# Attention with a log-multiplicity mask, sums from the exponential and inverse sums on the diagonal of the turning product; inject and lag stages reordered

## What is computed

```python
h = rmsnorm(x); u, q, k, v = split(h @ w_in)        # 4 x 1024 columns
y = Re(C x) + D u, x = complex diagonal scan of B u # 64 groups, state 64
z = gelu(y); z = z * sigmoid(z @ w_glu)
for window, dilation in ((128, 1), (512, 4), (2048, 16)):
    o_i, lse_i = softmax attention over t, t-d, .., t-window
o = sum(softmax(lse)_i * o_i)                       # 8 heads of 128
x = x + concat(rmsnorm(z), rmsnorm(o)) @ w_out
x = x + hierarchical_moe(rmsnorm(x))                # 32 SwiGLU experts, top 2
```

## Time and profile before

| | before |
|---|---|
| runs, us | 2140.65, 2148.05, 2150.82 |
| profiled execution, us | 2141.37 |
| its span, us | 2139.6 |
| mean granted clock of PE | 0.931 |
| busy: PE, DVE, ACT, POOL | 83%, 27%, 15%, 13% |
| chain of work that ended last: DMA, PE, DVE | 37%, 30%, 6% |
| read from HBM | 517.78 MB |

### The profile page before, as it was taken

One profiled execution on the slowest core, in us unless ns is written; L12 is line 12 of the kernel. 1 busy time (PEld: TensorE's weight loads), 2 busy tenths in 40 slices (PEclk: granted clock), 3 DMA queues, 4 the chain that ended last, 5 costly groups with the idle time before them and its releaser, 6 DMA issues.

```text
span 2139.6 us, 26995 instructions
## 1 busy us (share of the span) xinstructions
PE 1772.0 (83%) x10906; PEld 1240.1 (58%) x10907; DVE 579.4 (27%) x1218; ACT 312.2 (15%) x505; POOL 273.9 (13%) x193
## 2 busy tenths in 40 slices
PE   7997999898559999997687787877877797977780
PEld 6887888787337888886444444444444454544440
DVE  6300899822976520002300000000000000000006
ACT  4002211002232201111110110101101010111012
POOL 0641322101920000000100000000000000000000
PEclk9998999999689999998799999989999999999996
DMA  5245212335904422332799999999999689899995
GB/s 226 79 116 121 70 62 116 118 137 148 6 28 153 176 100 83 133 119 72 313 395 411 400 422 400 407 388 396 411 401 393 269 331 413 335 404 417 409 420 223
DMA packets 92405, 536.13 MB, mean 251 GB/s; under 512 B 28760, under 2 KB 41560, under 8 KB 47256
## 3 DMA queue, kind: packets, MB, share of 16 engines
q1 hardware_dynamic: 74528, 514.07, 63.3%
q0 software_dynamic: 7776, 17.07, 2.6%
q10 hardware_dynamic: 10048, 4.23, 1.0%
HBM read 517.78 MB, written 30.91 MB: 256 GB/s over the span
## 4 chain that ended last, share of the span: by engine, by line
DMA 37%; PE 30%; DVE 6%; issue 2%; ACT 1%; SPq 0%; POOLq 0%; ACTq 0%; DVEq 0%
DMA arena<-w_up_in 35%; PE psum L528 13%; PE psum L797 10%; PE psum L813 2%; DVE arena L1300 1%; DMA arena<-y_rows 1%; PE psum L654 1%; DVE arena L1294 1%; DVE arena L1292 1%; PE psum L660 1%; PE psum L777 1%; PE psum L722 1%; DVE arena L1552 1%; DVE arena L1545 0%; DMA y_rows<-arena 0%
## 5 line engine op out<-in xcount | busy, mean ns | idle before, releaser
L528 PE MATMUL psum<-arena 128*128 128x260 f32 x3328 | 744.8, 387 | 26.5 <-ACT arena L835 13.0
L528 PEld LDWEIGHTS psum<-arena 128*128 128x128 f32 x3328 | 639.1, 192 | 128.3 <-issue 19.3
L797 PE MATMUL psum<-arena 128*64 128x256 f32 x4352 | 538.9, 406 | 178.5 <-DMA arena<-w_up_in 142.0
L797 PEld LDWEIGHTS psum<-arena 128*64 128x64 f32 x4352 | 331.0, 146 | 396.5 <-DMA arena<-w_up_in 166.1
L1538 DVE TENSOR_TENSOR arena<-arena,psum 128x256 f32<-128x256 f32 x34 | 14.3, 421 | 953.5 <-PE psum L797 953.5
L813 PE MATMUL psum<-arena 128*64 128x512 f32 x1088 | 245.4, 603 | 20.4 <-ACT arena L994 15.6
L813 PEld LDWEIGHTS psum<-arena 128*64 128x64 f32 x1088 | 75.6, 138 | 168.3 <-issue 131.8
L1110 POOL DMA_INDIRECT y_rows<-arena x34 | 34.0, 1000 | 979.0 <-ACT arena L999 934.1
L994 ACT ACTIVATE arena<-psum 128x256 f32<-128x256 f32 x34 | 13.1, 384 | 496.8 <-PE psum L803 496.8
L777 PEld LDWEIGHTS psum<-arena 64*128 64x128 f32 x560 | 64.9, 203 | 22.1 <-issue 22.1
L777 PE MATMUL psum<-arena 64*128 64x64 f32 x560 | 69.7, 276 | 8.9 <-ACT arena L985 8.9
(11 more groups left out here) (295 smaller groups left out, 1127.2 us busy)
## 6 DMA issues: line engine op xcount, KB each, us to landing
arena<-w_down_in SPq DMA_DIRECT2D x64, 2048.0 KB, 27.3
arena<-w_gate_in SPq DMA_DIRECT2D x64, 2048.0 KB, 28.0
arena<-w_up_in SPq DMA_DIRECT2D x64, 2048.0 KB
arena<-w_in_in SPq DMA_DIRECT2D x32, 1024.0 KB, 4.8
arena<-w_out_in SPq DMA_DIRECT2D x16, 1024.0 KB, 4.8
arena<-k_cache_in SPq DMA_DIRECT2D x8, 1024.0 KB, 6.7
arena<-v_cache_in SPq DMA_DIRECT2D x8, 1024.0 KB, 4.8
arena<-y_rows SPq DMA_DIRECT2D x8, 1024.0 KB, 8.2
```

The costliest lines, as they stand in the source:

```text
L528: last = mm(pair(n)[:, h, :], w(kk), rhs(kk)[:, HALF * h:HALF * (h + 1)], start=(kk == begin), stop=(kk == kn - 1 and stop))
L797: last = mm(ps[64 * h:64 * h + 64, i // 2, 0:256], xtr[:, kk, :], w[:, kk, 256 * h:256 * (h + 1)], start=(kk == 0), stop=(kk == 15))
```

## The change

It does these things:

- The constant is one table, -log(n), with 1e30 where n is 0. DVE's mask becomes table - SCALE x scores, its minimum is the bias, and ACT exponentiates with scale -1, so n is inside the exponential. The exponential also gives the sum. DVE only inverts it; ACT writes the inverse on a diagonal (`inv_l`), and PE turns the weights by a real product with that diagonal instead of a transpose.
- ACT's copy of the turned weights and PE's weighing stand one step later.
- Rounds 0 and 1 of the weight stacks are issued by POOL.
- Key chunks go with tiles 26 to 31, and the last two behind them.
- `ssm_c` is loaded ahead of the stores of k and v; POOL waits for `bst` only at the last of the four powers, and uses another buffer for intermediate results until then.
- The lag kernels are made, copied and given their diagonal in two halves, and PE starts on a channel tile when its part is ready.
- Two semaphores that did nothing go.

```diff
--- before
+++ after
...
@@ -379,9 +380,11 @@
                         if keys is not None:
                             if a > keys:
                                 sp.wait_ge(s_ku, it * 2 + (j - 2 * keys - 1))
-                            sp.dma_start(kch[j].rearrange("p k d -> p (k d)"),
-                                         t["k_cache"][bass.ds(it * 2 + (j - 2 * keys), 1)].rearrange(
-                                             "o p n -> (o p) n")).then_inc(s_kch[j], 16)
+                            load_keys(j, it * 2 + (j - 2 * keys), 1)
+
+            def load_keys(j, c, n):
+                sp.dma_start(kch[j].rearrange("p k d -> p (k d)"),
+                             t["k_cache"][bass.ds(c, n)].rearrange("o p n -> (o p) n")).then_inc(s_kch[j], 16)
 
             load_tiles(2, 6)
             for rd in (2, 3):
...
@@ -393,13 +396,18 @@
                                      ).then_inc(s_bs[rd], 16)
             load_tiles(6, 8)
             sp.wait_ge(s_inj, 24)
-            sp.dma_start(view(tail, 1024), t["c_branch"]).then_inc(s_attc, 16)
+            sp.dma_start(branch, t["c_branch"]).then_inc(s_attc, 16)
             sp.dma_start(smp_const, t["c_sample"]).then_inc(s_sc, 16)
-            load_tiles(8, 11)
-            load_tiles(11, 12, 11)
-            load_tiles(12, 15, 11)
-            load_tiles(15, 16)
-
+            load_tiles(8, 13)
+            load_tiles(13, 14, 13)
+            load_tiles(14, 16, 13)
+            for c in (6, 7):
+                sp.wait_ge(s_ku, c - 1)
+                load_keys(c % 2, c, 1)
+
+            sp.wait_ge(s_proj, 32)
+            sp.wait_ge(s_state, 1)
+            sp.dma_start(cw[:, 0], t["ssm_c"]).then_inc(s_c, 16)
             sp.wait_ge(s_rope, 16)
             sp.dma_start(t["k_out"], k).then_inc(s_kout, 16)
             sp.wait_ge(s_rope, 24)
...
@@ -410,9 +418,6 @@
             sp.dma_start(router_const, t["c_router"]).then_inc(s_rc, 16)
             sp.dma_start(region("upper", P), t["c_upper"]).then_inc(s_rc, 16)
 
-            sp.wait_ge(s_proj, 32)
-            sp.wait_ge(s_state, 1)
-            sp.dma_start(cw[:, 0], t["ssm_c"]).then_inc(s_c, 16)
             sp.wait_ge(s_vout, 16)
             sp.wait_ge(s_vr, 8)
             sp.wait_ge(s_vs, 1)
...
@@ -611,7 +616,8 @@
                 if a >= 2:
                     pe.wait_ge(s_ptev, a - 1)
                 for j in range(a % 4 + 1):
-                    last = pe.transpose(ps[:, 4 + a % 2, P * j:P * (j + 1)], sc[a % 4][:, P * j:P * (j + 1)], ident)
+                    last = mm(ps[:, 4 + a % 2, P * j:P * (j + 1)], sc[a % 4][:, P * j:P * (j + 1)], inv_l[:, a % 4],
+                              start=True, stop=True)
                 last.then_inc(s_pt, 1)
 
             def weigh(h):
...
@@ -631,8 +637,9 @@
                 if a + 4 < 4 * NH:
                     scores(a + 4)
                 turn(a)
-                if a % 4 == 3:
-                    weigh(a // 4)
+                if a % 4 == 0 and a:
+                    weigh(a // 4 - 1)
+            weigh(NH - 1)
 
             pe.wait_ge(s_cw, 1)
             pe.wait_ge(s_msk, 4 * NH)
...
@@ -642,12 +649,13 @@
                         last = mm(ps[32 * r:32 * r + 32, ct // 4, P * (ct % 4):P * (ct % 4 + 1)].rearrange(
                             "p (j m) -> p j m", j=CHUNK), bst[:, ri, 4 * ct + r, :], cw[:, 0:CHUNK, ri, 4 * ct + r, :],
                             start=(ri == 0), stop=(ri == 1))
-            last.then_inc(s_lag, 1)
-
-            pe.wait_ge(s_lagd, 1)
+                if ct % 4 == 3:
+                    last.then_inc(s_lag, 1)
+
             pe.wait_ge(s_state, 1)
             for ct in range(8):
                 b = ct % 2
+                pe.wait_ge(s_lagd, ct + 1)
                 if ct >= 2:
                     pe.wait_ge(s_z, ct - 1)
                 for lag in range(CHUNK):
...
@@ -660,6 +668,8 @@
                             mm(yjc[b][32 * r:32 * r + 32, j, :], cw[:, j + 1, ri, i, :], xs[:, ri, i, 0:NCH],
                                start=False, stop=(j == CHUNK - 1 and ri == 1), skip_group_check=True)
                 ys = ps[:, 2 * b + 1, 0:NS]
+                if ct == 0:
+                    pe.wait_ge(s_lagc, 3)
                 mm(ys, lagk[:, ct, 0, :], u[:, ct, SEQ:T], start=True, stop=False, skip_group_check=True)
                 for ri in range(2):
                     for r in range(4):
...
@@ -845,13 +855,6 @@
             A(tmp[5], tmp[4], ACT.Sin).then_inc(s_lact, 1)
             A(tmp[6], tmp[4], ACT.Sin, scale=0.5).then_inc(s_lact, 1)
 
-            def stack_weights(rd):
-                for r in range(4):
-                    for j in range(CHUNK):
-                        act.dma_start(bws[rd % 2][32 * j:32 * j + 32, :, r, :],
-                                      bw[32 * r:32 * r + 32, CHUNK - 1 - j, rd // 2, 4 * (rd % 2):4 * (rd % 2) + 4, :]
-                                      ).then_inc(s_bs[rd], 16)
-
             def chunk_states(rd):
 
                 for b in range(6):
...
@@ -896,7 +896,12 @@
             def exps(a):
                 act.wait_ge(s_mx, a + 1)
                 w = P * (a % 4 + 1)
-                A(sc[a % 4][:, 0:w], sc[a % 4][:, 0:w], ACT.Exp, bias=stat[:, a:a + 1], scale=SCALE).then_inc(s_exp, 1)
+                A(sc[a % 4][:, 0:w], sc[a % 4][:, 0:w], ACT.Exp, bias=stat[:, a:a + 1], scale=-1.0,
+                  accum_out=stat[:, 32 + a % 4:33 + a % 4]).then_inc(s_exp, 1)
+
+            def diagonal(a):
+                act.wait_ge(s_inv, a + 1)
+                A(inv_l[:, a % 4], ident, ACT.Copy, scale=stat[:, 36 + a % 4:37 + a % 4]).then_inc(s_p, 1)
 
             def turned(a):
                 act.wait_ge(s_pt, a + 1)
...
@@ -914,17 +919,21 @@
             for a in range(4 * NH):
                 if a + 1 < 4 * NH:
                     exps(a + 1)
-                turned(a)
+                diagonal(a)
+                if a:
+                    turned(a - 1)
                 if a % 4 == 1 and a > 4:
                     head_out(a // 4 - 1)
+            turned(4 * NH - 1)
             head_out(NH - 1)
 
-            act.wait_ge(s_lag, 1)
             act.wait_ge(s_lagc, 1)
-            for r in range(4):
-                last = A(lagk[32 * r:32 * r + 32, :, :, 32 * r:32 * r + 32],
-                         psum_t[32 * r:32 * r + 32, 0:1024].rearrange("p (c j m) -> p c j m", c=8, j=CHUNK), ACT.Copy)
-            last.then_inc(s_lagc, 1)
+            for b in range(2):
+                act.wait_ge(s_lag, b + 1)
+                for r in range(4):
+                    last = A(lagk[32 * r:32 * r + 32, 4 * b:4 * b + 4, :, 32 * r:32 * r + 32],
+                             ps[32 * r:32 * r + 32, b, :].rearrange("p (c j m) -> p c j m", c=4, j=CHUNK), ACT.Copy)
+                last.then_inc(s_lagc, 1)
             for ct in range(8):
                 act.wait_ge(s_y, ct + 1)
                 if ct == 3:
...
@@ -1043,9 +1052,15 @@
                 complex_product(flat[kk], flat[kk - 1], (lre[:, 0:1024], lim[:, 0:1024]), two)
             tt(two[0][:, 0:1], two[0][:, 0:1], two[0][:, 0:1], ALU.mult).then_inc(s_bw, 1)
 
+            pool.wait_ge(s_bw, 1)
+            for rd in range(2):
+                for r in range(4):
+                    for j in range(CHUNK):
+                        pool.dma_start(bws[rd][32 * j:32 * j + 32, :, r, :],
+                                       bw[32 * r:32 * r + 32, CHUNK - 1 - j, 0, 4 * rd:4 * rd + 4, :]
+                                       ).then_inc(s_bs[rd], 16)
             pool.wait_ge(s_rstd, 1)
             pool.wait_ge(s_rc, 16)
-            pool.wait_ge(s_bw, 1)
             tt(cosr, cos, rstd, ALU.mult)
             link(tt(sinr, sin, rstd, ALU.mult))
             for m in range(24):
...
@@ -1074,7 +1089,10 @@
 
             lam = (over(lamp[:, 0]), over(lamp[:, 1]))
             for kk in range(1, CHUNK + 1):
-                complex_product((cw[:, kk, 0], cw[:, kk, 1]), (cw[:, kk - 1, 0], cw[:, kk - 1, 1]), lam, bt, True)
+                if kk == CHUNK:
+                    pool.wait_ge(s_c, 16 * 3)
+                complex_product((cw[:, kk, 0], cw[:, kk, 1]), (cw[:, kk - 1, 0], cw[:, kk - 1, 1]), lam,
+                                bt if kk == CHUNK else (cw[:, CHUNK, 0], cw[:, CHUNK, 1]), True)
 
             tr, ti = bt
             cr, ci = over(coef[:, 0]), over(coef[:, 1])
...
@@ -1289,18 +1307,13 @@
                 dve.wait_ge(s_sco, a + 1)
                 if a >= 4:
                     dve.wait_ge(s_pt, a - 3)
-                tt(sc[a % 4][:, 0:w], ps[:, qt, 0:w], branch_neg[:, 512 - w:512], ALU.add).then_inc(s_msk, 1)
+                stt(sc[a % 4][:, 0:w], ps[:, qt, 0:w], -SCALE, branch[:, 512 - w:512], ALU.mult, ALU.add).then_inc(s_msk, 1)
                 dve.wait_ge(s_msk, a + 1)
-                link(dve.tensor_reduce(stat[:, a:a + 1], sc[a % 4][:, 0:w], X, ALU.max))
-                ts(stat[:, a:a + 1], stat[:, a:a + 1], -SCALE, None, ALU.mult).then_inc(s_mx, 1)
```

(15 more changed lines are left out.)

21 lines of the change are left out of this document (9 added, 12 removed).

## The result

| | before | changed |
|---|---|---|
| median of runs, us | 2149.44 (4 runs) | **2065.20** (4 runs: 2061.01, 2062.41, 2067.99, 2068.49) |
| ratio, 95% interval | | **0.9614** [0.9579, 0.9649] |
| profiled execution, us | 2141.37 | 2068.49 |
| its span, us | 2139.6 | 2066.7 |
| mean granted clock of PE | 0.931 | 0.944 |

The account below looks back on a forecast made before the run. Expert weights streaming at DMA rate bound the later half, untouched; waits ahead of it were to shrink. Gains of 9.5, 11.4, 46.3 and 4.5 (71.7) from 2141.4 gave 2069.7; 2.3 added for 2072 us, range 2056 to 2096.

Parts of the forecast that it names:

- A, inject: Inject stage: POOL issues 32 weight stacks, ACT only those of u; ends near 171.5 instead of 181.0, 9.5 us gained.
- B, keys: Projection tiles: with keys from tile 26 on, tile 25's load comes in time; 11.4 us gained, 8.6 at least.
- C, attention and POOL: Attention to lag stage: shorter heads and POOL's earlier start bring the lag stage to T0 + 73.4, 46.3 us gained.
- D, lag: Lag stage: working in halves cuts 10.1 us to 4.8; 4.5 gained after a deduction, bounds 3.5 and 7.
- I take 1.1, nearer to the indirect ones' own duration: Inject: assumed POOL issue time per copy in us, between its indirect copies' 1.31 start to start and ACT's 0.78.
- the wait of 4 us that I gave as a sign: Inject: expected sign that inject(1) waits some 4 us for POOL's stacks.
- from 132 to 147: Inject: ACT issues only the copies of u between these times in us, landed by 151.
- The rival of dear issues: Inject: POOL issues at 2 us each give 2101 us, chance 0.09; at 4 us each 2165, chance 0.03.
- The rival of a low clock: Attention: PE's clock stays low; mean 0.7 gives 2094 us, chance 0.10; 0.5 throughout gives 2118, chance 0.06.
- The rival of the held mask: Attention: POOL still holds up DVE's new mask, 1.2 us more on 32 masks; 2085 us, chance 0.06.
- The rival that a turning product costs four transposes: Attention: a head takes 10.4 us and attention ends 19.6 us late; 2092 us, chance 0.04.
- less some 0.8 because PE now waits 2 us for POOL just ahead: Lag stage: deduction in us from a gain of 5.3, leaving 4.5.

Follow-up runs that it names:

- both edits: Changed kernel with POOL's state-weight products before its fourth power, and its second half of copies held until half of u's landed: 2063.34 us, ratio 0.9644.
- the second experiment: Changed kernel with the cached keys loaded from tile 22 on again, as before the change: 2079.56 us, ratio 0.9699.
- the pair of extra passes: Changed kernel with one more unused DVE pass per attention step, one run each: 2081.17 us reading SBUF, 2069.51 us reading PSUM.
- the second profile of before: The kernel before, unchanged, run again for one more profile: 2147.35 us, span 2145.5.
- the control: The changed kernel as it is, timed again beside two further variants, five runs: 2066.97 us, ratio 0.9660 to before.

## Why the prediction was right

The forecast was 2072, the median came at 2065.2. In the profiled execution's terms it was 2069.7, and that came at 2068.5. Term by term, against the first profile of before:

| term | predicted | measured in the trace |
|---|---|---|
| A, inject | 9.5 (2 to 14) | 13.6 |
| B, keys | 11.4 (8.6 at least) | 11.6 |
| C, attention and POOL | 46.3 (39 to 48) | 46.0 |
| D, lag | 4.5 (3.5 to 7) | 6.7 |
| sum, at the start of GLU | 71.7 | 77.8 |
| behind GLU | 0 | -4.9, scatter |

**A was mis-sized** in the step "I take 1.1, nearer to the indirect ones' own duration": POOL issued in 0.55, below even the bound of 0.78 that came from ACT. Neither row was a bound: one is of an indirect copy, the other of a different engine's queue, and 0.78 is a mean at that, with a median of 0.62 for the 32. So inject(1) didn't wait for POOL's stacks at all, and the wait of 4 us that I gave as a sign isn't there. What did limit was a term I had taken as unchanged, ACT's copies of u "from 132 to 147": they ran to 156.5, beside POOL's stream and the load of weights. The windows of 128 to 158 us, of before and of the changed kernel:

```profile
128.00:158.00 30.00, 30.00 (x138) 25.87 (x137) 4.27 (x25) 0.00 (x0) 3.21 (x4) 1.00 0.61 158
```

```profile
128.00:158.00 30.00, 30.00 (x138) 25.77 (x136) 4.23 (x25) 1.45 (x3) 20.22 (x35) 1.00 0.98 211
```

The DMA share went from 0.61 to 0.98. 13.6 came close to the 14 that the prediction gave as a limit, but not for the reason that it gave, PE at the pace of ACT's copies out of PSUM. PE is busy all through the stage, and takes 7.65 us for it also where both edits are in, while ACT waits for the first group in the one and there has three lined up, which it copies 0.44 apart instead of 0.70. So the 13.6 are 11.9 us less of idle time (1.85 for 13.73) and 1.6 of clock, 7.65 at a granted clock of 1.00 where before's stage takes 9.20 at 0.83; the prediction had no term for the clock here. That the u copies slow down because POOL's stream runs beside them is shown by the experiments with the copies back on ACT and with POOL's second half behind (0.66 to 0.92 each in the first; 0.66 in the second between POOL's two halves, 0.82 to 1.09 in the other groups). What the two streams share, no run tells. That the engines are full can't be the whole of it: in before the last four copies of u take 0.66 each in a window with a DMA share of 1.26 and 186 GB/s (164.5 to 168.5), in the changed kernel 1.18 each at 1.15 and 189 GB/s (151.0 to 155.8, when POOL has issued its last and some of its copies haven't landed), and the experts' weights move at 379 GB/s with a share of 0.95. The rival of dear issues falls with the 0.55, and so does the Trainium skill's figure as a price of issuing ("DMA: Bandwidth & Descriptors", "Latency and other measured facts", about 1 us to the first byte from GpSimd). It is a time to the first byte, and here POOL issues the next copy after 0.55.

**B** came as worked out; the second experiment undid it for the same amount.

**C** came within 0.3 us, and by the mechanism given: the mask was not held (0.69), heads took 7.70 (with DVE busy 4.09 and PE 7.18 where 4.9 and 7.5 were worked out), PE ended at T0 + 70.8 (71.3), POOL began at T0 + 6.6 (6.2) and ended at T0 + 73.7 (73.3), PE waited 2.85. The rival of a low clock falls: it is 1.00 in the head. The rival of the held mask falls with the pair of extra passes. These rows agree with what the Trainium skill, "SBUF — State Buffer", "SBUF: two separate sides", says of a VectorE operation with two SBUF inputs and a GpSimd one that reads SBUF, that one blocks the other: here 1.59 against 0.69, with POOL slowed in turn. The number of SBUF inputs is not the whole condition, though. In before the scaling L1303, whose only full-width input lies in SBUF, takes 1.92 at 512 columns while POOL works (mean of four, 534 to 604 us) and 0.49 after it, more of a hold than that of L1300 (1.66 and 0.69), while the maximum L1294 over as many columns in SBUF takes 0.69 in both. The rival that a turning product costs four transposes falls by the lengths of its groups in PE's timeline:

```profile
497.64 0.49 PE L619 MATMUL psum<-arena 128*128 128x128 f32 x2 [1.36 <-ACT arena L904]
499.02 0.71 PE L619 MATMUL psum<-arena 128*128 128x128 f32 x4 [0.46 <-ACT arena L904]
507.87 0.94 PE L619 MATMUL psum<-arena 128*128 128x128 f32 x6 [0.38 <-ACT arena L904]
```

Two passes more, one product, cost 0.22; the old transposes cost 0.11 each (0.66 for four, 0.44 for two at 607.08 us in the same trace). Twice, not four times as the Trainium skill has it for FP32 ("TensorE: Matmul & The Clock Gate", Terms).

**D was undersized** in the step "less some 0.8 because PE now waits 2 us for POOL just ahead". The wait of 2.85 didn't bring the clock down: the first eight products of y took 2.39 where before's took 3.92, and 1.5 came on top instead of 0.8 off. The experiments have both sides: 2.39 behind 1.3 us of idle, 3.81 behind 4.50. The prediction's 2.2 for later groups of y was a misreading: in before they take 2.32 and 2.42. One rival's sum was off as well. With the mask held, six heads at 9.7 end at T0 + 67.9, so attention would have ended near T0 + 85 and not T0 + 87, 2 us less than the 2085 given; it changes no verdict.

The sum was 6.1 short (3.3 against the second profile of before), the scatter behind GLU took 4.9 back, and so the profiled execution met the forecast more closely than its terms did. That is luck of the run: between medians, 2149.44 and 2065.20, the gain is 84.2, and between those measured beside the control, 2141.28 and 2066.97, it is 74.3. The terms of the trace, 77.8 and 75.0, stand between.

## What to carry to other kernels

Where two engines share a resource, the windows with the partner busy and idle, side by side, tell which operations to remove; count the form of an operation (where its operands lie) before its length, and let PSUM be an operand. When two engines must both finish before a stage, work out both ends: here the new attention alone was worth 31 of 46 us and the earlier start of POOL gained nothing until attention was short. Price an issue on an engine that has never issued plain copies with a wide interval downwards too, and ask what the new stream does to the other one, which you call unchanged.

## What the runs showed of the hardware

- A plain SBUF to SBUF copy of 64 KB is issued by POOL in 0.55 us, in ACT's queue in 0.71 to 0.78 on average (22.63, 23.74 and 24.93 for 32), 0.62 at the median: ACT's mean is high by a few slow ones, up to 1.91. Landing took 5.3 at the median from POOL, beside ACT's copies of u, and 2.6 from ACT alone.
- ACT's copies of u (128 KB) took 0.66 to 0.92 us each without POOL's stream and 1.1 to 1.4 beside it, by groups of four.
- The hold between DVE and POOL goes both ways: 0.69 to 1.59 on DVE, 1.92 to 2.22 and 2.36 to 2.69 on POOL. A scaling from SBUF to SBUF is held (0.49 to 1.92), a maximum or minimum over a row in SBUF isn't (0.69 in both).
- After 13.7 and 12.2 us of idle PE's first inject stage took 9.20 and 9.56 us (clock 0.83 and 0.79), after 2.79 us 9.32 (0.82), after 2.66 and 1.85 us 7.65 (1.00). The eight first products of y: 2.39 after 1.3 us of idle (1.00), 3.81 after 4.5 (0.61). Attention's first steps ran at full speed in one profile of the changed kernel (0.71 for two turning products) and at half in the other (1.09), with the same wait ahead of them; there it cost nothing, since POOL ended later.
